# The word for the token numbers laid out behind the working area instead of ahead of it

## The chip, the cores and the metric

The kernel runs on one core of a Trainium2 chip. The metric is the time of one execution in device microseconds; the time of a kernel is the median of several executions. One further execution was taken by the profiler, and its trace is what is read here. In the rows PE is TensorE's matmul, PEld its weight load, DVE VectorE, ACT ScalarE, POOL GpSimd, and SP the engine that issues most of the DMAs.

## The reference

One inference step of a two-layer decoder, in float32, for a prompt of 256 tokens and for 8 requests of one token each; together T = 264 token columns, D = 1024 wide. Cut to what matters:

```
for l in range(2):
    q, k, v, z, xbc, dt = split(x @ w_in[l])             # 1024 x 3080
    m  = concat(diff_attention(q, k, v), ssd(xbc, dt) * silu(z)) @ w_out[l]
    x  = LN(alpha * x + m)
    x  = LN(alpha * x + cross_attn(x, mem_k, mem_v, w_cq[l], w_co[l]))
    if l == 0:
        h = silu(x @ w_ffn_gate) * (x @ w_ffn_up)        # 1024 x 2816 each
        c = h @ w_ffn_down                               # 2816 x 1024
    else:
        gate = softmax over the top 2 of x @ w_router    # 8 experts
        c = sum over e of swiglu(x, w_exp_gu[e], w_exp_down[e]) * gate[:, e]
    x = LN(alpha * x + c)
```

Keys, values, convolution and state caches are outputs too.

## The kernel before

All work is laid out by hand, engine by engine, with semaphores; no scheduler orders anything. The program first names areas of the on-chip memory (`sb`): a ring of six slots of 16 KB per partition for weights and caches, `xT`, `R`, `SQ`, `memT` (activations, features on the partitions), constants, small statistics, `mem_rows`, `slot_token`, and last `arena`, the working area of 16248 words per partition. The areas are laid one behind the other, each begun at a multiple of 32 bytes.

`arena` has no fixed use. `carve` hands out stretches of it, stage by stage, so that the same bytes serve one after another: rows of q, k, v, z and the attention probabilities; keys, scores and probabilities of the cross-attention; `x_high`, `x_low`, `h_high`, `h_low` and the two `first_high` buffers of the dense feed-forward of layer 0; `x_tok`, `Sel`, `xg_high`, `xg_low`, `he_high`, `he_low`, `ye_high`, `SelT` and the sum `acc` of the experts of layer 1; and `y_tok` at the end.

In the two feed-forward parts each float32 operand is split into a high part and a remainder, and a product is three matmuls: high with high, high with low, low with high. The weights' high part goes to the buffers `high` (in `R`, `SQ`, `memT`) or, for the first chunk of the dense part, to `first_high` (in `arena`); their remainder overwrites the ring slot (`ring_low`). ScalarE makes the high parts (L1772, L1849), VectorE the remainders (L2155, L2273).

- Dense part: the weights are TensorE's loaded operand (`high`, `first_high`, `ring_low`), the 264 columns of `x_high[k]`, `x_low[k]` or of `h_high[f]`, `h_low[f]` are streamed. `mm` at L1216 records every matmul; a row `bank<-x_high,high` names the streamed operand first and the loaded one second. For each of 11 chunks `f` the loops run over two halves `j`, four groups (two blocks of columns `b`, gate and up `u`) and four `kk` with `k = 4*j + kk`, three matmuls each: 96 matmuls a chunk, 48 a half.
- Experts: 8 passes of one loop body. The gathered tokens `xg_high`, `xg_low` (later `he_high`, `he_low`) are the loaded operand, 512 columns of weights are streamed from `high` or `ring_low`. An expert has 11 x 8 x 3 = 264 such matmuls for gate and up and 22 x 2 x 3 = 132 for down, so 396, and the eight have 3168. Two matmuls of 264 columns per block add the previous expert's rows to `acc` (`SelT` streamed, `ye_high` and `ye_low` loaded).

`slot_token` holds one 32-bit word per partition: the number of the token in each slot of the next expert. VectorE writes it once an expert (L2176); GpSimd then issues the indirect DMA (L973) that gathers the next expert's token rows into `xT`; TensorE transposes these rows late in the same expert.

Byte addresses per partition in the program as built: `ring` 16512, `xT` 114816, `R` 123264, `SQ` 131712, `memT` 140160, `mem_rows` 162176, `slot_token` 164224, all multiples of 64; `arena` 164256, which is 32 past one. A row of 264 words has 1056 bytes, 16.5 times 64, so of `x_high[k]` (from 210720) the rows with even `k` begin 32 past a multiple of 64 and those with odd `k` on one; `h_high`, `h_low` and `x_low` alternate in the same way. Rows of 128, 512 and 1024 words in `arena` (`xg_high`, `he_high`, `first_high`, `ye_high`, `y_tok`) all begin 32 past.

Of the kernel before, what the change touches and what calls it, by code (L numbers as in the profile page):

```python
# [27 lines left out]
I32 = mybir.dt.int32  # L28
# [4 lines left out]
P = 128  # L33
# [354 lines left out]
def build(nc, a, outs, lots=SLOTS, always=False):  # L388
# [3 lines left out]
    with ExitStack() as ctx:  # L392
        begins = {}

        def sb(name, shape, dt=F32):
            tensor = ctx.enter_context(nc.sbuf_tensor(name, shape, dt))
            begins[name] = nc.sbuf_base - 4 * math.prod(shape[1:])
            return tensor
# [42 lines left out]
        cnt = sb("cnt", [1, 1])  # L441
        cnti = sb("cnti", [1, 1], I32)
        mem_rows = sb("mem_rows", [P, 512])
        slot_token = sb("slot_token", [P, 1], I32)
        x_rows = nc.dram_tensor("x_rows", [T, D], F32).ap()
        arena = sb("arena", [P, ARENA])
        banks = [ctx.enter_context(nc.psum_tensor(f"bank{i}", [P, 512], F32)) for i in range(8)]

        used = [0]
# [2340 lines left out]
```

## Time and profile before

| | us |
|---|---|
| median of 3 executions | 1812.07 (1811.1 to 1814.3) |
| the profiled execution | 1809.09 |
| its span, first to last instruction | 1807.2 |
| PE busy in the span | 1760.1 (97%) |
| DVE busy | 1225.6 (68%) |
| ACT busy | 852.8 (47%) |

The span is what the trace covers; 1.9 us of the profiled execution lie around it. PE's share is a share of time in which a matmul was under way, and matmuls overlap: it is not PE at its peak. The granted clock of TensorE over the span is 0.993 of full speed.

### The profile page before, as it was taken

The numbers are of one execution on the slowest core, as the hardware profiler recorded it, in microseconds if no ns is written. First come the engines' busy times: TensorE is split into PE (matmuls) and PEld (weight loads), VectorE is DVE, ScalarE is ACT, GpSimd is POOL, SyncE is SP. The second block draws the span as 40 slices with busy tenths as digits, with TensorE's granted clock in tenths as the row PEclk, the third lists the DMA queues.
The fourth block names the chain that finished last, engine by engine and source line by source line (L and its number), as shares of the span: only waits on it lengthen the run. The fifth ranks groups of instructions, "written<-read, shape, count | busy, mean of one in ns | idle before, by whom it ended". The sixth has DMA issues, their size and how long they took to land.

```text
span 1807.2 us, 24014 instructions
## 1 busy us (share of the span) xinstructions
PE 1760.1 (97%) x8760; PEld 1360.8 (75%) x8760; DVE 1225.6 (68%) x1739; ACT 852.8 (47%) x978; POOL 112.2 (6%) x120
## 2 busy tenths in 40 slices
PE   7999999999999999999999999999999999999998
PEld 4646587789999565568677878878888878878786
DVE  2687636255544288543626989898988989898984
ACT  1122211154442122302205777777777777777774
POOL 0530000000000332000001000000000000000000
PEclk9999999999999999999998999999999999999999
DMA  9556544845526455563682989999999999999980
GB/s 323 183 199 212 215 185 169 285 158 181 175 83 228 137 185 171 187 262 123 233 279 96 358 279 356 345 348 352 349 376 324 377 324 363 337 350 352 348 335 26
DMA packets 300436, 459.34 MB, mean 254 GB/s; under 512 B 10879, under 2 KB 213817, under 8 KB 300343
## 3 DMA queue, kind: packets, MB, share of 16 engines
q1 hardware_dynamic: 294630, 442.63, 71.6%
q0 software_dynamic: 3424, 11.50, 1.9%
q10 hardware_dynamic: 2304, 4.20, 0.6%
q8 instruction: 47, 0.77, 0.2%
q14 instruction: 31, 0.25, 0.0%
HBM read 444.97 MB, written 13.46 MB: 254 GB/s over the span
## 4 chain that ended last, share of the span: by engine, by line
PE 86%; DVE 7%; ACT 3%; issue 1%; DMA 1%; SPq 1%; POOL 0%; ACTq 0%; DVEq 0%; POOLq 0%
PE bank L1216 83%; PE bank L1220 3%; DVE arena L2682 1%; DVE ring_low L2155 1%; ACT high L1772 1%; DMA out<-mem_rows 1%; DVE R L2296 1%; ACT L1772 0%; ACT arena L1840 0%; POOL arena L964 0%; ACT ye_high L1808 0%; ACT SQ L1861 0%; DVE st L2654 0%; DVE st L2575 0%; SPq L727 0%
## 5 line engine op out<-in xcount | busy, mean ns | idle before, releaser
L2155 DVE TENSOR_TENSOR ring_low<-ring,high 128x2048 fp32r<-128x2048 f32 x264 | 603.0, 2292 | 87.0 <-ACT high L1772 84.0
L1772 ACT ACTIVATE high<-ring 128x2048 fp32r<-128x2048 f32 x264 | 505.3, 1917 | 110.7 <-PE bank L1216 101.5
L1216 PE MATMUL bank<-high,xg_high 128*128 128x512 f32 x704 | 285.0, 405 | 6.2 <-DVE ring_low L2155 5.8
L1216 PE MATMUL bank<-ring_low,xg_high 128*128 128x512 f32 x704 | 278.5, 396 | 0.0
L1216 PE MATMUL bank<-high,xg_low 128*128 128x512 f32 x704 | 278.2, 395 | 0.0
L1216 PEld LDWEIGHTS bank<-high,xg_high 128*128 128x128 f32 x704 | 132.4, 188 | 36.3 <-DVE ring_low L2155 7.3
L1216 PEld LDWEIGHTS bank<-ring_low,xg_high 128*128 128x128 f32 x704 | 132.2, 188 | 31.7
L1216 PEld LDWEIGHTS bank<-high,xg_low 128*128 128x128 f32 x704 | 132.5, 188 | 28.4
L1840 ACT ACTIVATE arena<-bank 128x512 f32<-128x512 f32 (+3 forms) x95 | 46.4, 525 | 218.4 <-PE bank L1216 142.8
L1216 PE MATMUL bank<-high,he_high 128*128 128x512 f32 x352 | 141.8, 403 | 0.0
L1216 PE MATMUL bank<-ring_low,he_high 128*128 128x512 f32 x352 | 139.2, 396 | 0.0
L1216 PE MATMUL bank<-high,he_low 128*128 128x512 f32 x352 | 139.1, 395 | 0.0
L2273 DVE TENSOR_TENSOR ring_low<-ring,high 128x2048 fp32r<-128x2048 f32 (+1 forms) x32 | 71.1, 2225 | 92.6 <-ACT high L1849 92.6
L1216 PE MATMUL bank<-xT,ring 128*128 128x264 f32 x512 | 120.3, 391 | 0.8 <-ACT xT L1876 0.8
L1216 PE MATMUL bank<-SQ,ring 128*128 128x264 f32 x512 | 116.6, 391 | 0.9 <-issue 0.7
L1216 PE MATMUL bank<-ring,xT 128*128 128x512 f32 x256 | 116.5, 613 | 0.0
L1216 PE MATMUL bank<-ring,memT 128*128 128x512 f32 x256 | 113.3, 595 | 0.0
L1216 PEld LDWEIGHTS bank<-SQ,ring 128*128 128x128 f32 x512 | 98.1, 192 | 18.7 <-DVE SQ L2643 0.9
L1216 PEld LDWEIGHTS bank<-xT,ring 128*128 128x128 f32 x512 | 95.2, 190 | 21.9 <-issue 4.4
L1216 PE MATMUL bank<-x_high,ring_low 128*128 128x264 f32 x352 | 99.9, 284 | 0.0
L1849 ACT ACTIVATE high<-ring 128x2048 fp32r<-128x2048 f32 (+1 forms) x32 | 59.6, 1864 | 82.9 <-PE bank L1216 82.0
L1216 PEld LDWEIGHTS bank<-ring,xT 128*128 128x128 f32 x256 | 49.3, 196 | 62.6 <-issue 62.5
(327 smaller groups left out, 2613.2 us busy)
## 6 DMA issues: line engine op xcount, KB each, us to landing
ring<-in_w_exp_gu SPq DMA_DIRECT2D x176, 1024.0 KB, 11.3
ring<-in_w_exp_down SPq DMA_DIRECT2D x40, 2048.0 KB, 14.2
ring<-in_w_in SPq DMA_DIRECT2D x12, 2048.0 KB, 9.7
ring<-in_w_ffn_gu SPq DMA_DIRECT2D x22, 1024.0 KB, 8.5
ring<-in_w_ckv SPq DMA_DIRECT2D x8, 2048.0 KB, 8.6
ring<-in_cache_mem_k SPq DMA_DIRECT2D x16, 1024.0 KB, 8.1
ring<-in_cache_mem_v SPq DMA_DIRECT2D x16, 1024.0 KB, 6.6
ring<-in_cache_attn_k SPq DMA_DIRECT2D x32, 256.0 KB, 3.5
```

Of the source, the lines that this page charges most:

```text
L1216: return M.matmul(out, lhsT, rhs, start=start, stop=stop)
L1220: return M.transpose(out, in_, ident[0:n, 0:n])
L1772: S.activation(high_bufs[h % HIGH_BUFS][:], ring[:, s, j * HALF:(j + 1) * HALF], ACT.Copy).then_inc(split_high, 1)
L1840: emptied_after(name, S.activation(dst, src(bk), func))
L1849: S.activation(high, ring[:, s, part], ACT.Copy).then_inc(ffn_high, 1)
L2155: V.tensor_tensor(ring_low[:, s, part], ring[:, s, part], high_bufs[h % HIGH_BUFS][:], ALU.subtract).then_inc(split_low, 1)
L2273: V.tensor_tensor(ring_low[:, s, part], ring[:, s, part], high, ALU.subtract).then_inc(ffn_low, 1)
L2296: V.scalar_tensor_tensor(R[:, k, :], R[:, k, :], col_g(l, i, k), stat[:], ALU.mult, ALU.mult).then_inc(scaled.sem, 1)
L2682: ins = V.scalar_tensor_tensor(ctmp[:, (2 * t + j) * MD:(2 * t + j + 1) * MD], Kb[:, t, h * MD:(h + 1) * MD], 1.0, bk[:, j * MD:(j + 1) * ...
```

## The change

`slot_token` is named after `arena` instead of before it.

```
         mem_rows = sb("mem_rows", [P, 512])
-        slot_token = sb("slot_token", [P, 1], I32)
         x_rows = nc.dram_tensor("x_rows", [T, D], F32).ap()
         arena = sb("arena", [P, ARENA])
+        slot_token = sb("slot_token", [P, 1], I32)
```

In the built program `arena`, with all that is carved from it, begins at 164224 instead of 164256, and `slot_token` lies at 229216. Every engine has the same instructions in the same order as before (3372 rows on PE, 1177 on DVE, 617 on ACT, 97 on POOL, 560 on SP, none moved); only addresses differ. The rows of 128, 512 and 1024 words now begin on a multiple of 64; of the rows of 264 words those with even numbers do, and those with odd numbers begin 32 past.

## Rows read from the trace of the kernel before

**Rows 1.** The page: span, busy time, and the chain that ended last by line.

```profile
span 1807.2 us, 24014 instructions
...
PE 1760.1 (97%) x8760; PEld 1360.8 (75%) x8760; DVE 1225.6 (68%) x1739; ACT 852.8 (47%) x978; POOL 112.2 (6%) x120
...
PE bank L1216 83%; PE bank L1220 3%; DVE arena L2682 1%; DVE ring_low L2155 1%; ACT high L1772 1%; DMA out<-mem_rows 1%; DVE R L2296 1%; ACT L1772 0%; ACT arena L1840 0%; POOL arena L964 0%; ACT ye_high L1808 0%; ACT SQ L1861 0%; DVE st L2654 0%; DVE st L2575 0%; SPq L727 0%
```

**Rows 2.** Busy time by stretch: the second of the eight experts.

```profile
core 0: us, PE busy (x) PEld busy (x) DVE busy (x) ACT busy (x) POOL busy (x), PEclk, DMA share, GB/s
...
1083.59:1183.95 100.36, 99.52 (x457) 80.92 (x457) 89.62 (x78) 74.82 (x64) 1.03 (x1) 1.00 1.03 350
```

**Rows 3.** The chain in order of time (start, us, what): 24 matmuls of an expert.

```profile
1102.81 5.60 PE bank L1216 x24
```

**Rows 4.** Who waited for whom in the experts, 983 to 1787 us: PE's own wait.

```profile
PE bank L1216 <- DVE ring_low L2155: 5.8, 7, 0.8
```

**Rows 5.** Timeline of PE, dense part; every third matmul from 392.44 on.

```profile
386.60 0.28 PE L1216 MATMUL bank<-x_high,first_high 128*128 128x264 f32 x1
...
392.44 0.28 PE L1216 MATMUL bank<-x_high,high 128*128 128x264 f32 x1
...
392.80 0.28 PE L1216 MATMUL bank<-x_high,high 128*128 128x264 f32 x1
...
393.16 0.28 PE L1216 MATMUL bank<-x_high,high 128*128 128x264 f32 x1
...
393.53 0.28 PE L1216 MATMUL bank<-x_high,high 128*128 128x264 f32 x1
...
393.89 0.28 PE L1216 MATMUL bank<-x_high,high 128*128 128x264 f32 x1
...
394.26 0.28 PE L1216 MATMUL bank<-x_high,high 128*128 128x264 f32 x1
...
394.62 0.28 PE L1216 MATMUL bank<-x_high,high 128*128 128x264 f32 x1
...
394.98 0.28 PE L1216 MATMUL bank<-x_high,high 128*128 128x264 f32 x1
...
395.35 0.28 PE L1216 MATMUL bank<-x_high,high 128*128 128x264 f32 x1
```

**Rows 6.** Groups by line and shape (busy us, mean ns): same work, different areas.

```profile
L1216 PEld LDWEIGHTS bank<-high,xg_low 128*128 128x128 f32 x704 | 132.5, 188 | 28.4
...
L1216 PEld LDWEIGHTS bank<-x_high,ring_low 128*128 128x128 f32 x352 | 66.1, 188 | 0.0
...
L2064 ACT ACTIVATE h_high<-mem_rows 128x264 fp32r<-128x264 f32 x11 | 4.7, 426 | 21.3 <-DVE mem_rows L2741 21.3
L2064 ACT ACTIVATE h_high<-arena 128x264 fp32r<-128x264 f32 x11 | 4.7, 426 | 0.0
L2741 DVE TENSOR_TENSOR arena<-arena,bank 128x264 f32<-128x264 f32 x11 | 4.7, 423 | 0.0
L2741 DVE TENSOR_TENSOR mem_rows<-mem_rows,bank 128x264 f32<-128x264 f32 x11 | 4.6, 422 | 0.0
```

**Rows 7.** DMA issues: count, KB each, median us from issue to landing.

```profile
ring<-in_cache_mem_v SPq DMA_DIRECT2D x16, 1024.0 KB, 6.6
...
out<-mem_rows ACTq DMA_DIRECT2D x16, 256.0 KB, 4.9
...
arena<-out SPq DMA_DIRECT2D x4, 1024.0 KB, 4.9
...
out<-arena POOLq DMA_DIRECT2D x8, 256.0 KB, 2.6
...
xT<-x_rows,slot_token POOLq DMA_INDIRECT x8, 7.6
```

**Rows 8.** Timeline, POOL and PE: the gather of the first expert and its transposes.

```profile
1028.32 1.16 POOL L973 DMA_INDIRECT xT<-x_rows,slot_token  x1 [69.25 <-DVE slot_token L2176]
...
1067.28 1.04 PE L1220 MATMUL bank<-const,xT 128*128 128x128 f32 x8
```

More of the change, by code:

```diff
@@ L443, in build @@
         mem_rows = sb("mem_rows", [P, 512])
-        slot_token = sb("slot_token", [P, 1], I32)
         x_rows = nc.dram_tensor("x_rows", [T, D], F32).ap()
         arena = sb("arena", [P, ARENA])
+        slot_token = sb("slot_token", [P, 1], I32)
         banks = [ctx.enter_context(nc.psum_tensor(f"bank{i}", [P, 512], F32)) for i in range(8)]
```

## The prediction

> **What bounds the kernel now.** I read the page first: the chain that ended last lies to 83% on one line of PE, the matmuls of L1216 [rows 1]. Then the busy time of one expert: PE is under way in 99.52 of 100.36 us, at a granted clock of 1.00 (the 2.4 GHz level), while DVE has 89.62 and ACT 74.82 [rows 2]. Eight such experts are about 803 of the 1807.2 us. The waits there show PE waiting for anything but itself in only 7 places, 5.8 us together [rows 4]. So an expert takes what its matmuls take, and the place to look is the time of one matmul: 24 of 512 columns go by in 5.60 us, 233 ns each [rows 3]. The DMA share in the same stretch is 1.03 at 350 GB/s [rows 2]: the transfers have no spare time either, though PE is not seen to wait for them.
>
> The change moves no instruction. What can change is only what an instruction costs when an operand begins on a multiple of 64 bytes instead of 32 past one. The trace of before holds both kinds side by side, since all areas except the arena begin on a multiple of 64, and within the arena rows of 264 words alternate. So each kind of access can be priced without leaving this trace.
>
> **The change, part by part.**
>
> *Loaded operand of TensorE* (3168 matmuls of the experts: `xg_high`, `xg_low`, `he_high`, `he_low` go from 32 past to a multiple of 64). The weight load itself takes 188 ns from the arena (`xg_low`, 32 past) and 188 ns from the ring (`ring_low`, on a multiple) [rows 6]. Whether the period of the matmuls feels it is seen in the dense part. Its first chunk takes two of three loaded operands from `first_high`, 32 past: the 48 matmuls of its second half run from 386.60 to 392.44, 5.84 us, 121.7 ns each. From the second chunk on, all loaded operands begin on a multiple: from 392.44 to 395.35 there are eight starts three matmuls apart, so 24 in 2.91 us, 121.25 ns [rows 5]. The difference of 0.42 ns, put on the two thirds that changed, is 0.63 ns per load, hardly more than the 0.01 us to which starts are given (0.4 ns over 24). These matmuls are 121 ns apart, less than the 188 ns that a load lasts, so loads follow each other more closely here than in the experts (233 ns apart): if the load's address mattered, here it would show. I take 0. As the end for a gain: 0.63 ns, scaled up by columns 512/264 to 1.2 ns, times 3168, is 3.9 us.
>
> *Streamed operand of TensorE.* In the experts it is `high` or `ring_low`, which don't move. In the dense part it is `x_high`, `x_low`, `h_high`, `h_low`, of which one half of the rows begins on a multiple of 64 before and the other half after: the two halves change places. Even a real price would cancel. The rows also show that there is none: from 392.44 on `k` runs 0, 1, 2, 3 and again, and the blocks of three last 0.36, 0.36, 0.37, 0.36, 0.37, 0.36, 0.36, 0.37 us; the four even ones (32 past) sum to 1.46 us, the four odd ones (on a multiple) to 1.45 [rows 5]. That is 0.8 ns per matmul at most. 0.
>
> Here the Trainium skill has a rule ("SBUF — State Buffer", section Specifications): the memory is read in lines of 16 bytes, and going to a new line costs. Both 164256 and 164224 are multiples of 16, so by it no operand touches one line more or less, and the sum is 0. If lines of 64 bytes counted instead, a loaded row of 128 words (512 bytes) would touch 9 lines before and 8 after; a load that went by lines would then fall from 188 to 167 ns. The 188 ns from both addresses [rows 6] speak for the page and against that.
>
> *ScalarE and VectorE.* The rounding copy L2064 takes 426 ns whether it reads `mem_rows` (a multiple) or the arena's row (32 past); the multiplication L2741 takes 423 ns with both operands in the arena, 422 with both in `mem_rows` [rows 6]. 0, and at 1 ns in 423 it would be 0.2% of instructions that in the experts lie under PE's 99.52 us. The cover here is that DVE has 89.62 us of 100.36 [rows 2]; it would take 10 us more an expert before VectorE set the end.
>
> *DMAs into and out of the arena.* Loads of 1024 KB land 4.9 us after issue in the arena and 6.6 us in the ring; stores of 256 KB out of the arena land after 2.6 us, out of `mem_rows` after 4.9 us [rows 7]. Queues differ, so the pairs are no clean comparison, but nothing shows the arena as slow. Only the store of `y_tok` at the very end lies on the path; a gain there is bounded by the duration of such a store, 2.6 us, and a loss is not to be seen. I take 0.
>
> The skill's "DMA: Bandwidth & Descriptors", section How a descriptor splits into AXI transactions, gives a price of its own: reads begin at the 256-byte boundary below the start, in beats of 32 bytes. A row of 4096 bytes from the arena started 160 past such a boundary and now starts 128 past, 133 beats against 132. By that, an estimate, a store of 2.6 us gains 0.02 us. No row resolves it.
>
> *`slot_token` itself.* Its word moves from a multiple of 64 to 32 past one. VectorE writes it, GpSimd reads it for the gather. The gather is issued at 1028.32 and lands after 7.6 us, at about 1036; the transposes that need it start at 1067.28 [rows 7, 8]. Some 31 us cover any change of its cost; without that cover, 1 us more for each of eight gathers would be 8 us. 0.
>
> **The sum** is 0: the profiled execution's 1809.09 us stay (1807.2 span and 1.89 around it). The median of the runs is 1812.07, 2.98 us (0.16%) above that execution, so on the measure that counts I forecast 1812. Bounds: 3.9 us of gain from the loads; for a loss 0.8 ns per 264 columns, scaled to 512 and taken 3168 times, 4.9 us (below). With the spread of the runs themselves, 1811.1 to 1814.3, that is about 1806 to 1818. A difference under 0.2% (3.6 us) can't be told from none.
>
> **The rivals.**
>
> *Faster: the matmuls of 512 columns carry an excess because of the address.* 512 columns at one per clock would take 213 ns at 2.4 GHz; they take 233 [rows 3]. If those 20 ns came from loads that begin 32 past, PE would gain 3168 x 20 ns = 63 us. But then the transfers bind: an expert's weights are 3 x 1024 x 2816 x 4 bytes = 34.6 MB, at 350 GB/s [rows 2] 98.9 us against 100.36, 1.5 us less, eight times 12 us. That gives 1800. Against it: 264 columns at one per clock would be 110 ns, and they take 121.25 with every load on a multiple of 64 [rows 5], the same excess of about a tenth. It goes with the columns, not with the load's address. 0.10.
>
> *Slower: loaded and streamed operand now begin at the same place of a 64-byte line.* In the experts the loaded operand was 32 past and the streamed one on a multiple; now both are on a multiple, and two reads that run at once might collide. In the odd blocks of rows 5 both already begin there, and these are no slower than the even ones (1.45 against 1.46 us); what rounding leaves is 0.8 ns per matmul, for 512 columns 1.55 ns, times 3168 it is 4.9 us: 1817. From 1.1 ns a matmul on it decides the sign (3.6 us by 3168). 0.07.
>
> *The change doesn't do what it says.* It does: the base moves by 32 bytes. That it does nothing to the time is the forecast, 0.83.
>
> **How the numbers follow.** No difference 0.83, its own range 1808 to 1816; faster 0.10 (1800 and around); slower 0.07 (1817 and above). The range 1806 to 1818 holds the first case and the near part of both others. Faster by over 0.2%: 0.10; within: 0.83; slower: 0.07.
>
> **What the profile after would show.** The 24 matmuls of the chain again in 5.59 to 5.61 us, an expert in 100.3 us, the weight load at 188 ns from `xg_low`; in the dense part 121 to 122 ns a matmul in the first chunk and the second. The forecast is wrong if an expert's period differs from 100.36 us by over 0.4 us: shorter with 24 matmuls under 5.5 us would be the faster rival, longer with 24 over 5.63 us the slower one; a period that moves with the matmuls unchanged would be a wait that I haven't seen.

## The result and the profile after

The changed kernel takes 1798.42 us (median of 5 executions, 1794.58 to 1802.92) against 1812.07 before (by now also 5 executions, with the median and limits that the first 3 had): a ratio of 0.9923, interval 0.9901 to 0.9946. So it is faster by 0.8%, and outside the forecast range of 1806 to 1818. The profiled execution took 1795.52 us, with a span of 1793.7, which is 13.5 us less than in [rows 1].

The page of the changed kernel shows the same instructions and the same busy engines as [rows 1], with 15 us less of PE:

```profile
span 1793.7 us, 24014 instructions
...
PE 1745.0 (97%) x8760; PEld 1360.0 (76%) x8760; DVE 1224.9 (68%) x1739; ACT 853.0 (48%) x978; POOL 111.9 (6%) x120
```

The chain in order of time (start, us, what) shows an expert between two blocks of 28 matmuls: the first of the second expert (1082.89), of the third (1181.36) and of the eighth (1673.59). Between them stand runs of 24, which [rows 3] has at 5.60 us. The first row is the first block of the first expert, the last row is the adding of the eighth expert's rows, behind its matmuls:

```profile
990.88 5.96 PE bank L1216 x28
...
1082.89 6.24 PE bank L1216 x28
...
1101.70 5.48 PE bank L1216 x24
...
1113.11 5.50 PE bank L1216 x24
...
1130.91 5.47 PE bank L1216 x24
...
1181.36 6.24 PE bank L1216 x28
...
1673.59 6.24 PE bank L1216 x28
...
1767.37 5.22 PE bank L1216 x28
```

The same blocks before (first expert, second, eighth, and the adding behind it):

```profile
989.85 6.08 PE bank L1216 x28
...
1083.63 6.35 PE bank L1216 x28
...
1685.63 6.35 PE bank L1216 x28
...
1781.29 5.22 PE bank L1216 x28
```

From 1082.89 to 1673.59 six experts go by in 590.70 us, 98.45 each; before, from 1083.63 to 1685.63, in 602.00 us, 100.33 each. Each expert gains 1.88 us over 396 matmuls, 4.8 ns a matmul; the runs of 24 say 5.47 to 5.50 against 5.60, 4 to 5.5 ns. The busy time of the second expert stands beside [rows 2] (columns as there), and below it the stretch 340 to 345 us:

```profile
1082.89:1181.36 98.47, 97.47 (x457) 80.81 (x458) 89.53 (x78) 74.83 (x64) 1.03 (x1) 1.00 1.05 357
340.00:345.00 5.00, 4.99 (x15) 4.03 (x16) 0.00 (x0) 0.00 (x0) 0.00 (x0) 0.66 1.08 355
```

DVE and ACT work as long as before; PE is under way 2.05 us less; the granted clock is 1.00 in both. The transfers moved with it, from 350 to 357 GB/s. Who waited for whom in the experts (us in total, times, longest) gives PE the same seven waits as [rows 4], 1.2 us longer together:

```profile
PE bank L1216 <- DVE ring_low L2155: 7.0, 7, 1.0
```

All eight experts together, from the first row to the last, take 776.49 us instead of 791.44 and gain 14.95. Of that 1.03 us are lost ahead of the experts and 0.42 behind them, which leaves the 13.5 of the span. Ahead of them the granted clock is 0.66 between 340 and 345 us, where it was 1.00 before: for a part of that stretch TensorE was at its 1.2 GHz level, having been under way for 3.75 of the 5 us ahead of it (before, 4.10). The kernel with 128 bytes more (below), which gains nothing, shows 0.66 in that stretch too, after 4.11 of 5 us, so this isn't the saving's price.

The weight load of `xg_low` in the experts (groups by line and shape) lasts as long as before, and in the dense part nothing moved, as PE's timeline of the places of [rows 5] shows:

```profile
L1216 PEld LDWEIGHTS bank<-high,xg_low 128*128 128x128 f32 x704 | 132.5, 188 | 25.4
```

```profile
387.68 0.28 PE L1216 MATMUL bank<-x_high,first_high 128*128 128x264 f32 x1
...
393.49 0.28 PE L1216 MATMUL bank<-x_high,high 128*128 128x264 f32 x1
...
396.41 0.28 PE L1216 MATMUL bank<-x_high,high 128*128 128x264 f32 x1
```

48 matmuls of the first chunk take 5.81 us (before 5.84), 121.0 ns each, and the next 24 take 2.92 (before 2.91), 121.7. What became shorter is only the time from one 512-column matmul to the next.

### The profile page after: what moved, and what is told of

It is laid out like the page before. It is cut to its first block, busy times and chain, and to the rows that moved or that the text cites. A ratio compares the mean times of both kernels' runs of the same rounds, so it can differ in the third digit from the quotient of the medians.

```text
span 1793.7 us, 24014 instructions
## 1 busy us (share of the span) xinstructions
PE 1745.0 (97%) x8760; PEld 1360.0 (76%) x8760; DVE 1224.9 (68%) x1739; ACT 853.0 (48%) x978; POOL 111.9 (6%) x120
## 4 chain that ended last, share of the span: by engine, by line
PE 86%; DVE 7%; ACT 3%; issue 1%; DMA 1%; POOL 0%; SPq 0%; ACTq 0%; DVEq 0%; POOLq 0%
PE bank L1216 83%; PE bank L1220 3%; DVE arena L2682 1%; DVE ring_low L2155 1%; ACT high L1772 1%; DMA out<-mem_rows 1%; DVE R L2296 1%; ACT L1772 1%; ACT arena L1840 0%; POOL arena L964 0%; ACT ye_high L1808 0%; ACT SQ L1861 0%; DVE st L2654 0%; DVE st L2575 0%; DMA ring<-in_x_sample 0%
## 5 line engine op out<-in xcount | busy, mean ns | idle before, releaser
L1216 PE MATMUL bank<-high,xg_low 128*128 128x512 f32 x704 | 274.4, 390 | 0.0
```

The source lines that it names most:

```text
L1216: return M.matmul(out, lhsT, rhs, start=start, stop=stop)
```

## The experiments

Five readings were held against each other. **A**: a loaded operand that begins on a multiple of 64 bytes is the gain. **B**: what counts is whether loaded and streamed operand begin at the same place of a 64-byte line. **C**: other engines' or the DMAs' accesses to the arena became cheaper. **D**: what counts is the distance between loaded and streamed operand, modulo 256 bytes (or 128). **E**: the effect needs the other engines at work beside PE.

All layouts come from two edits: `carve(n)`, which takes `n` words of `arena` ahead of an area, and a `pad` of 8 words ahead of `ring`, which moves every later area by 32 bytes. The streamed operands (`ring`, and `high` in `R`, `SQ`, `memT`) lie a multiple of 256 bytes from each other, so one distance serves for all.

**Loads alone.** Before, with the loaded operands moved to a multiple of 64 and the rest of `arena` left 32 past:

```
+        carve(8)
         xg_high = parts_in("xg_high", "arena", used[0], [KT, P])
...
+        carve(8)
         sg = carve(2 * GU).rearrange("p (s n) -> p s n", s=2)
...
+        carve(8)
         he_high = parts_in("he_high", "arena", used[0], [FT, P])
...
+        carve(8)
         ye_at = used[0]
```

> The kernel before, with the four operands that TensorE loads in the experts (xg_high, xg_low, he_high, he_low) moved by 8 words so that they begin on a multiple of 64 bytes; all else in the arena stays 32 past one. Theory A (the address of the loaded operand sets the period of the 512-column matmuls): the whole gain, an expert in 98.4 to 98.5 us instead of 100.35, 24 matmuls of the chain in 5.45 to 5.49 us, about 1797 us. Theory B (what counts is that loaded and streamed operand begin at the same place of a 64-byte line): the same as A here. Theory C (other accesses to the arena, by VectorE, ScalarE or DMA, gave the gain): nothing, an expert in 100.35 us and 1812 us.

**Loads put back.** The same four lines in the changed kernel, so that its loads are off a multiple of 64 again and all else keeps the change:

> The changed kernel, with only those four loaded operands moved by 8 words, so that they begin 32 past a multiple of 64 bytes again; the rest of the arena stays on a multiple. A and B: the whole gain is lost, an expert in 100.35 us, 24 matmuls in 5.59 us, 1811 us. C: the gain stays, 98.45 us an expert and 1798 us.

**All 32 past.** The changed kernel with every area moved by 32 bytes:

```
+        sb("pad", [P, 8])
```

> The changed kernel with 8 words laid ahead of the ring, so that everything moves by 32 bytes: loaded and streamed operands of the experts both begin 32 past a multiple of 64. A: slow as before or worse, an expert in 100.35 us or more (more if the streamed address costs too), 1812 us or more. B: fast as the changed kernel, 98.45 us an expert, 1798 us.

**Streams 32 past.** The same pad in the kernel before, which puts the loads on a multiple of 64 and the streams 32 past one:

> The kernel before with the same 8 words ahead of the ring: the loaded operands now begin on a multiple of 64, the streamed ones (high, ring_low) 32 past. A: fast, 98.45 us an expert if the streamed address costs nothing, 1798 us. B: slow, 100.35 us an expert, 1812 us.

These four left A, B and C without support. Loads on a multiple of 64 gain nothing by themselves (0.9991), and the changed kernel keeps its whole gain with every operand 32 past (0.9902). B would give "loads alone" the gain too, since both operands then begin on a multiple of 64. C falls with "all 32 past" too: its `arena` begins at 164256, the very address of before, and the gain is whole. The other way round, with the loads put back `arena` keeps its new base and the gain is gone (1.0006). What the one gaining layout shares with the change is the distance from `ring` to `xg_high`, 163072 bytes, 637 times 256. So D was formed, after these four runs, and tried three times, with one line ahead of `xg_high` each.

**Before, distance 256:** `carve(56)` in the kernel before. `arena` stays 32 past a multiple of 64; the distance becomes a multiple of 256.

> The kernel before with 56 words left free ahead of xg_high, so that xg_high, xg_low, he_high and he_low (and what is carved behind them) lie a multiple of 256 bytes from the ring and the high buffers; the arena itself still begins 32 past a multiple of 64. D by 256 and D by 128: the whole gain, an expert in 98.45 us, 1798 us. If the arena's own place counts: none, 1812 us.

**After, 128 more:** `carve(32)` in the changed kernel; every operand stays on a multiple of 64.

> The changed kernel with 32 words (128 bytes) left free ahead of xg_high: all loaded and streamed operands of the experts still begin on a multiple of 64, at a distance of 128 past a multiple of 256. D by 256: the gain is lost, an expert near 100.2 us, about 1811 us. D by 128: it stays, 98.45 us and 1798 us.

**After, 256 more:** `carve(64)`.

> The same with 64 words (256 bytes). D by 256 and by 128: the gain stays, 98.45 us an expert, 1798 us. If the distance counts by a longer measure or only the one place of the changed kernel is good: lost, 1811 us.

| kernel | `ring` | `xg_high`, `he_high` | distance past a multiple of 256 | one expert, us | ratio to before |
|---|---|---|---|---|---|
| before | 16512 | 179616, 191904 | 32, 32 | 100.33 | 1 |
| changed | 16512 | 179584, 191872 | 0, 0 | 98.45 | 0.9923 [0.9901, 0.9946] |
| loads alone | 16512 | 179648, 192000 | 64, 128 | 100.31 | 0.9991 [0.9982, 1.0001] |
| loads put back | 16512 | 179616, 191968 | 32, 96 | 100.47 | 1.0006 [0.9993, 1.0019] |
| all 32 past | 16544 | 179616, 191904 | 0, 0 | 98.45 | 0.9902 [0.9885, 0.9918] |
| streams 32 past | 16544 | 179648, 191936 | 32, 32 | 100.33 | 0.9995 [0.9982, 1.0008] |
| before, distance 256 | 16512 | 179840, 192128 | 0, 0 | 98.45 | 0.9923 [0.9907, 0.994] |
| after, 128 more | 16512 | 179712, 192000 | 128, 128 | 100.20 | 0.9997 [0.9984, 1.0009] |
| after, 256 more | 16512 | 179840, 192128 | 0, 0 | 98.45 | 0.9918 [0.9895, 0.9941] |

An expert's time is that of six, between the chain's blocks of 28 as above. The chain's first run of 24 after 1100 us, in the seven kernels in the order of the table from "loads alone" on (the line of `mm` differs with the lines added):

```profile
1107.33 5.59 PE bank L1220 x24
```

```profile
1107.39 5.60 PE bank L1220 x24
```

```profile
1105.54 5.49 PE bank L1217 x24
```

```profile
1109.95 5.59 PE bank L1217 x24
```

```profile
1101.06 5.48 PE bank L1217 x24
```

```profile
1104.65 5.59 PE bank L1217 x24
```

```profile
1103.62 5.49 PE bank L1217 x24
```

There are only two groups, 5.59 to 5.60 and 5.48 to 5.49 us, and the distance alone sorts them. Sharpest is the pair "loads alone" and "before, distance 256": the same kernel before, the loads on a multiple of 64 in both, the streams too, and only the second has the distance and the gain. D by 128 falls with "128 more". That operands begin on a multiple of 64 is not what counts.

**A burst by address**, in the changed kernel after the last expert, with no other work beside PE: 48 matmuls for each width, shift of the loaded and shift of the streamed operand, whose results nothing uses. It was profiled once. Core of the edit:

```
+                loaded = he_high[:].rearrange("p f n -> p (f n)")
+                for cols, at, to in [...]:
+                    for n in range(48):
+                        mm(X_BANKS[1][:, 0:cols], loaded[:, at + P * (n % 3):at + P * (n % 3 + 1)],
+                           high_bufs[2][:, to + 512 * (n % 3):to + 512 * (n % 3) + cols], True, True)
+                    warm(X_BANKS[0], 1)
```

> The changed kernel with a burst of 2000-odd extra matmuls after the last expert, results unused, while the other engines idle: 48 matmuls for each choice of columns and of the places where loaded and streamed operand begin, one small matmul of constants between two choices. It only measures; its total time is longer by the burst, some 450 us. The runs so far speak against A, B and C: what is left is theory D, that the distance between loaded and streamed operand counts by a measure longer than 64 bytes (fast with a distance that is a multiple of 256, or of 128, slow at 32 or 64 past). D by 256: with 512 columns about 227 ns a matmul where the loaded operand is shifted by 0, 256 or 512 bytes, 232 to 235 ns at shifts of 32, 64, 128, 192 and 384; shifting the streamed operand by 32 bytes costs the same, and shifting both gives it back; with 264 columns no shift matters. D by 128: 227 ns also at 128 and 384. Theory E (the cost needs other engines or transfers at work): no difference by place anywhere in the burst.

PE's timeline (start, us for 48 matmuls). The first five rows have the loaded operand 0, 32, 128, 240 and 256 bytes from a multiple of 256; then come 264 columns at 0, 32 and 128 bytes; then 512 columns with the streamed operand shifted by 4, 16, 32 and 256 bytes, and with both operands shifted by 32; last 264 columns with the streamed operand shifted by 32. Below it stands the busy time of the burst (columns as in [rows 2]):

```profile
1770.39 11.28 PE L1225 MATMUL bank<-high,he_high 128*128 128x512 f32 x48
...
1816.50 11.54 PE L1225 MATMUL bank<-high,he_high 128*128 128x512 f32 x48
...
1863.04 11.49 PE L1225 MATMUL bank<-high,he_high 128*128 128x512 f32 x48
...
1909.29 11.27 PE L1225 MATMUL bank<-high,he_high 128*128 128x512 f32 x48
...
1920.64 11.28 PE L1225 MATMUL bank<-high,he_high 128*128 128x512 f32 x48
...
1966.61 6.12 PE L1225 MATMUL bank<-high,he_high 128*128 128x264 f32 x48
...
1979.01 6.12 PE L1225 MATMUL bank<-high,he_high 128*128 128x264 f32 x48
...
1991.40 6.27 PE L1225 MATMUL bank<-high,he_high 128*128 128x264 f32 x48
...
2016.34 11.79 PE L1225 MATMUL bank<-high,he_high 128*128 128x512 f32 x48
...
2028.21 11.47 PE L1225 MATMUL bank<-high,he_high 128*128 128x512 f32 x48
...
2039.76 11.54 PE L1225 MATMUL bank<-high,he_high 128*128 128x512 f32 x48
...
2074.39 11.28 PE L1225 MATMUL bank<-high,he_high 128*128 128x512 f32 x48
...
2109.29 11.28 PE L1225 MATMUL bank<-high,he_high 128*128 128x512 f32 x48
...
2155.54 6.21 PE L1225 MATMUL bank<-high,he_high 128*128 128x264 f32 x48
```

```profile
1772.00:2180.00 408.00, 408.00 (x2012) 345.37 (x2011) 0.00 (x0) 0.70 (x1) 0.00 (x0) 1.00 0.00 1
```

E falls: from 1772 to 2180 us DVE is not busy at all, ACT for 0.70 us, and the DMA share is 0.00, yet PE alone shows the effect, 0.26 us over 47 gaps, 5.5 ns a matmul. At 512 columns the pattern returns after 256 bytes, from either operand's side, and a shift of both by 32 costs nothing: it is the distance, as long as both operands begin on a multiple of 32 bytes. Off that, the distance doesn't say all: with the stream shifted by 16 the 48 matmuls take 11.47 us, with the load shifted by 240, which is the same distance modulo 256, only 11.27.

The expectation that at 264 columns no shift matters did not come: a shift of the load by 32 bytes costs nothing there, but one by 128 costs 0.15 us over 47 gaps, 3.2 ns a matmul, and a shift of the stream by 32 costs 0.09 us, 1.9 ns. The prediction was priced at this width, and its two stretches of the dense part couldn't have shown a distance anyway: rows of `x_high` lie 1056 bytes apart, so there the distance moves on by 32 bytes with each `k`, and both stretches mix several.

**Columns and neighbours.** The same frame, also profiled once, with nine widths at distances 0, 32 and 128, and 512 columns with shifts that alternate from one matmul to the next:

```
+                for cols, load, stream in [...]:
+                    for n in range(48):
+                        at, to = load[n % 2] + P * (n % 3), stream[n % 2] + 512 * (n % 3)
+                        mm(X_BANKS[1][:, 0:cols], loaded[:, at:at + P], high_bufs[2][:, to:to + cols], True, True)
...
```

> The changed kernel with 32 bursts of 48 matmuls after the last expert, whose results nothing uses. First question, which widths feel the distance between loaded and streamed operand: 256, 320, 416, 448, 480, 496, 504, 508 and 512 columns, each at a multiple of 256 bytes, 32 bytes past one and 128 past one. Theory 'longer than the load' (a load lasts 188 ns; matmuls closer than that are bound by other things): no difference up to 416 columns (189 ns), one that appears at 448 and reaches 227 against 233 at 512. Theory 'whole rows' (only 512 columns, 2048 bytes): 448 to 508 columns read the same at the three distances, 0.455 ns a column (204, 219, 226, 230, 231 ns), and 512 alone falls, to 227. Second question, which pair of operands meets, at 512 columns. Burst A: load and stream of a matmul are shifted together, by 0 and 32 bytes in turn, so its own pair is a multiple of 256 apart and each stream is 32 bytes off the load of the next matmul. Burst B: the load is shifted against its own stream, and lies a multiple of 256 from the stream of the matmul before. If a matmul's own pair counts: A 227, B 233 ns. If the stream and the next matmul's load, which runs under it, count: A 233, B 227. If either suffices for harm: both 233. Burst C is A with 256 bytes in place of 32: 227 by all. With the load alone shifted on every second matmul, and with the stream alone: half of the matmuls lose by either theory, 230 ns.

PE's timeline again: 416 columns at 0, 32 and 128 bytes, 448 at 0 and 128, 480 at 0 and 128, 496 at 0, 32 and 128; then 512 columns at 0 and at 32, burst A, burst B, burst C, the load alone shifted on every second matmul, the stream alone:

```profile
1809.05 9.39 PE L1225 MATMUL bank<-high,he_high 128*128 128x416 f32 x48
...
1818.53 9.47 PE L1225 MATMUL bank<-high,he_high 128*128 128x416 f32 x48
...
1828.07 9.32 PE L1225 MATMUL bank<-high,he_high 128*128 128x416 f32 x48
...
1837.47 10.09 PE L1225 MATMUL bank<-high,he_high 128*128 128x448 f32 x48
...
1857.82 10.14 PE L1225 MATMUL bank<-high,he_high 128*128 128x448 f32 x48
...
1868.04 10.74 PE L1225 MATMUL bank<-high,he_high 128*128 128x480 f32 x48
...
1889.69 10.90 PE L1225 MATMUL bank<-high,he_high 128*128 128x480 f32 x48
...
1900.68 11.07 PE L1225 MATMUL bank<-high,he_high 128*128 128x496 f32 x48
...
1911.83 11.23 PE L1225 MATMUL bank<-high,he_high 128*128 128x496 f32 x48
...
1923.14 11.07 PE L1225 MATMUL bank<-high,he_high 128*128 128x496 f32 x48
...
2002.93 11.27 PE L1225 MATMUL bank<-high,he_high 128*128 128x512 f32 x48
...
2014.27 11.54 PE L1225 MATMUL bank<-high,he_high 128*128 128x512 f32 x48
...
2037.52 11.58 PE L1225 MATMUL bank<-high,he_high 128*128 128x512 f32 x48
...
2049.18 11.46 PE L1225 MATMUL bank<-high,he_high 128*128 128x512 f32 x48
...
2060.72 11.27 PE L1225 MATMUL bank<-high,he_high 128*128 128x512 f32 x48
...
2072.07 11.62 PE L1225 MATMUL bank<-high,he_high 128*128 128x512 f32 x48
...
2083.78 11.45 PE L1225 MATMUL bank<-high,he_high 128*128 128x512 f32 x48
```

All widths from the same timeline, us for 48 matmuls:

| columns | 0 bytes | 32 bytes | 128 bytes |
|---|---|---|---|
| 256 | 6.10 | 6.03 | 6.11 |
| 320 | 7.38 | 7.39 | 7.39 |
| 416 | 9.39 | 9.47 | 9.32 |
| 448 | 10.09 | 10.10 | 10.14 |
| 480 | 10.74 | 10.75 | 10.90 |
| 496 | 11.07 | 11.23 | 11.07 |
| 504 | 11.25 | 11.37 | 11.52 |
| 508 | 11.28 | 11.39 | 11.34 |
| 512 | 11.27 | 11.54 | 11.54 |

On the widths neither theory came out. A difference of 0.05 us is 1 ns a matmul; a choice that was run in both bursts came out within 0.01 us, and within 0.05 at 128 bytes. "Only whole rows" is wrong, since at 504 columns 32 bytes cost 2.6 ns and 128 cost 5.7. "Longer than the load" is not borne out either: there is no one width from which the distance counts. It shows at 416 columns (up to 3.2 ns, the best distance there is 128 and not 0), hardly at 448, where it was expected to appear (1 ns), at 480 for 128 bytes alone, at 496 for 32 bytes alone; and in the burst before it showed at 264 columns for 128 bytes, though matmuls of 264 columns follow each other every 120 ns and a load lasts 188.

On the neighbours, A and B both lose (6.6 and 4.0 ns a matmul), and C doesn't. With the load alone shifted on every second matmul the cost is 7.4 ns, and not the half of 5.7 that was expected; with the stream alone it is 3.8 ns, nearer to the half. In A, in B and with the load alone, each matmul has either its own load or the next one's off its stream, never both, and all three lose. With the stream alone every second matmul has both off and the others neither. This fits that either is enough for harm, but it isn't shown: in the first three the loads also alternate by 32 bytes among themselves, and no burst takes that apart. Nor does it say which of the two reads waits.

## Why the prediction was wrong

The step that failed is "Loaded operand of TensorE", in two places. It priced an operand's address by itself, while what counts is its distance from the streamed one. And it took the price from matmuls of 264 columns with the words "if the load's address mattered, here it would show", because they follow each other more closely than a load lasts. That doesn't hold: in the burst a load shifted by 32 bytes costs nothing at 264 columns and 5.5 ns at 512. Its two stretches also mixed distances, so their difference priced none. The 0.63 ns found there, scaled by columns to 1.2, stand against 4.8 ns that each of the 3168 matmuls of 512 columns gained. The term was 0 with an end of 3.9 us; it measured 14.95. The scale by columns was the weak step: it took for granted that what a wide matmul pays can be read from a narrow one.

*Streamed operand.* The 0 for the dense part held (121.0 and 121.7 ns). In the experts "which don't move" was true and not enough, since the other end of the distance moved.

*The rule on 16-byte lines* of the Trainium skill ("SBUF — State Buffer", section Specifications) gave 0. Both addresses are multiples of 16 and the time changed all the same; the rule doesn't speak against a further one, but as a sum for this change the measurement decides. A second statement of the Trainium skill bears on the cause: "TensorE: Matmul & The Clock Gate", section Step-by-step: what each phase is for, has TensorE read streamed and loaded operand through two independent ports, so that loading takes nothing from a running matmul. At 320 columns the runs agree with that (7.38 to 7.39 us at all three distances); at 512 they don't: the same two reads cost 5.5 ns more by their distance alone.

*ScalarE and VectorE, the DMAs, `slot_token`.* All 0, and nothing contradicts them: DVE is busy 89.53 us in an expert against 89.62, the part behind the experts grew by 0.42 us, and "loads put back" keeps the moved word and the moved base and is as slow as before (1.0006).

*The faster rival* (0.10) had the place and nearly the time, 1800 against 1798.42, and its sign, 24 matmuls under 5.5 us, came but for a few runs at 5.50. Its reasons were wrong twice. Of the excess of 20 ns over one column per clock only some 5 come from the addresses, and by their distance, not by loads that begin 32 past. And the transfers, which were to cap the gain at 350 GB/s, went to 357; their share of 1.03 went along with PE's pace and was no limit at it. Two errors of opposite sign met near the right number.

*The slower rival* had the right kind of cause, the place of the loaded operand against that of the streamed one, with the modulus and the sign wrong: at the same place modulo 256 is the good case, and its price was again scaled from 264 columns.

## What to carry to other kernels

Where 512-column float32 matmuls set the pace, as here, look at the address of the loaded operand minus that of the streamed one; a few words of padding that make it a multiple of 256 were worth 0.8% of this kernel. When an operand moves, price the pair and not the operand, and take the price from matmuls of the same width: a narrower one may show nothing at the same shift. A layout change that moves no instruction can still move the time, so a padded version of both kernels is a cheap control.

## What the runs showed of the hardware

For 128 x 128 loads and 512 streamed columns of this type, the mean time between the starts of single matmuls in the burst by address, its first four left out, goes with the shift of the loaded operand like this:

| bytes | 0 | 4 | 8 | 32 | 64 | 96 | 128 | 192 | 224 | 240 | 256 | 288 | 384 | 512 |
|---|---|---|---|---|---|---|---|---|---|---|---|---|---|---|
| ns | 227.2 | 232.5 | 230.5 | 233.2 | 233.4 | 234.2 | 232.3 | 228.8 | 233.3 | 226.9 | 227.3 | 233.2 | 233.4 | 227.2 |

No theory had foreseen that 192 and 240 are nearly as good as 0, or that even the best case keeps 14 ns over the 213 that one column per clock would take. A streamed operand that begins 4 or 16 bytes past a multiple of 256, with the load on one, gives 238.5 and 231.8 ns: off a multiple of 32 the distance alone doesn't fix the time. Why 256, why the good distance differs with the width, what starts off a multiple of 32 change, and where the 14 ns go stays open. A load shifted by 240 bytes in the whole kernel was not tried: 0.3 ns times 3168 is 1 us, too little to tell from no change.
